# Block two in a second layout: factors found in groups, queries left unnormalized, gate units inside the attention, and the next norm begun early

## The chip, the cores and the metric

One core of a Trainium2 chip runs the whole program. The metric is the device time of one execution in microseconds. Engines are named as the profile names them: PE (matmuls; PEld is its weight load), DVE (vector), ACT (scalar), POOL (GpSimd) and SP, which only issues DMAs.

## What is computed

Two blocks in a row, each of two layers, on 512 tokens of width 1024. Block one (dilated attention, a gated recurrence and two FFNs) is not touched, except for a load near its end. Block two is this, twice:

```python
h = _rmsnorm(x, norm_g[l]); z = h @ w_in[l]
(nsa_q, nsa_kv, nsa_gate, nsa_silu, fox_qkv, fox_f, fox_silu,
 mem_q, mem_silu, merge_g) = _split(z, IN_SPLITS)
# nsa: q = rope(rmsnorm(q)); three attentions: compressed keys, selected keys, window
# fox: q and k normalized, logits + c[q] - c[k], c = cumsum(log_sigmoid(f_logit + bias))
# mem: q and k normalized, softmax(q @ k_mem) @ v_mem
# each branch: (o * silu(gate part of z)) @ w_branch, times sigmoid(merge_g), summed
x = x + merged @ w_out
```

Heads are 64 wide (memory heads 128), so a tile of 128 rows holds two heads. Every head norm needs a mean of squares for each token and head.

## The kernel before

Activations lie feature by token, [128, 8, 512]. All weights come as 434 units of [128, 1024] in a fixed order (`unit_order`). SP loads a unit, POOL splits it into a high and a low part (`w_hi`, L1848; `w_lo`, four quarters, L1852), and PE multiplies high by high, high by low and low by high: 24 matmuls of 512 columns (L331 to L333) for a full unit. Three units are in flight. Each engine runs its own list of instructions in order; semaphores join them.

A layer of block two has four stages.

**Projections** (`pe_projections` and its twins on ACT and DVE). 35 units in slots m = 0 to 34, the products in banks m % 3. Eight of the slots (memory keys and values) have 256 columns in place of 512. 22 slots carry a head norm. For each of them ACT copies and squares the bank (L1175, L1178), PE sums the squares by token (L1113, "sums"), DVE finds the factor by 13 or 14 dependent tiny instructions (`dve_rsqrt`, L438 to L456, tile `ep_nar`), widens it (L1269, `ep_wide`), PE transposes it into bank 6 (L1125, "spread") and DVE multiplies (L1253). There is one set of sums in bank 7 at a time: PE waits for slot m's factor before it sums the next. Seven slots are then rotated (L1132, L1258 to L1261). Value slots are scaled by DVE (L1228) and transposed by PE (L1138). Woven between the slots: the compression of keys and values (64 matmuls each, L1326), the norm of the memory, and some 35 steps that make the forget term. What comes when is set by `later` and by generators, one or two steps a slot.

**Attention** (`pe_attend` and twins). Four chunks, n = 0 to 3, of 36 tasks. A task is a tile of 128 queries, one head, one kind. PE makes the logits, DVE finds the maximum, ACT the exponentials, PE transposes them two steps later, ACT copies them out, PE multiplies by the values four steps later (L1563), DVE stores with the factor five steps later. Queries of one head stand in a tile whose other half is zero (`nsa_q_half`), staged by DVE for each chunk. After a chunk the pipeline is emptied, three tiles of output are transposed back (L1521) and copied by ACT (L1595).

**Gates** (`pe_silu` and twins). 12 units; DVE scales, ACT takes SiLU (L1675), DVE multiplies by the attention's output (L1690), and ACT and DVE split into high and low.

**Merge**. 24 + 12 units, then 8 units of `w_out`, whose results DVE adds to the residual `x_res` (L1764). The next layer begins when the last of them is added (`layer_begins`).

## Time and profile before

| | us |
|---|---|
| median of 3 runs | 3389.7 (3380.18 to 3391.31) |
| the profiled execution, time / span | 3390.8 / 3389.3 |
| layer 0 of block two: start 1690.6, first rotation 1746.8, attention 2018.4, gates 2236.8, merge 2303.3 | |
| layer 1: start 2546.1, first rotation 2582.5, attention 2855.1, gates 3073.0, end 3389.3 | |

The stage times are read from the trace, from the last instruction of one stage to the first of the next on PE; the start of a layer is the end of the last matmul before it. The profile's PE time contains modelled ends: a matmul's row reaches over the beginning of the next, so a stretch can show more than PE does at its peak. In a window's row the stretch and its length come first, then the busy time of PE, PEld, DVE, ACT and POOL with their instructions, the granted clock, the DMA share and GB/s. The clock stands as a share of 2.4 GHz; 0.50 is 1.2 GHz.

### The profile page before, as it was taken

The page shows a single profiled execution, that of the slowest core. Times are in us where ns is not written, and L with a number is a line of the kernel's source. Part 1 is how long each engine was busy: PE and PEld are TensorE (multiplying, and loading weights), DVE is VectorE, ACT ScalarE, POOL GpSimd, SP SyncE. Part 2 cuts the span into 40 slices and gives each one's busy share as a digit, 9 for nine tenths or more (in the row PEclk, how much of TensorE's full clock was granted, in tenths as well). Part 3 has the DMA queues.
Part 4 walks back from the last instruction along what each step waited for, and adds up shares of the span by engine and source line. Part 5 has one row for each costly group of instructions (what it writes and reads, how often), then busy time and mean ns, then how long its engine had stood idle before and what let it go on. Part 6 is the DMA issues. An engine that isn't in the chain of part 4 may idle for free.

```text
span 3389.3 us, 42390 instructions
## 1 busy us (share of the span) xinstructions
PE 3157.9 (93%) x15466; PEld 2576.6 (76%) x15474; DVE 1654.8 (49%) x3680; ACT 792.4 (23%) x1755; POOL 1933.4 (57%) x2206
## 2 busy tenths in 40 slices
PE   7999998899998889999978799999998889999999
PEld 6777777788887767888767677788887767778887
DVE  2333334476603756663056666653325766665232
ACT  1111111222201422221021016641002112663100
POOL 5555553699976777998744540047774454005775
PEclk9999999899998999999978889999998888999999
DMA  3222221222231221222231220012223121001222
GB/s 138 89 87 84 95 91 44 69 94 94 94 100 63 74 81 69 94 94 97 100 108 49 70 69 1 1 48 96 94 100 112 50 75 56 2 1 62 95 95 86
DMA packets 66445, 255.74 MB, mean 75 GB/s; under 512 B 7616, under 2 KB 8128, under 8 KB 64320
## 3 DMA queue, kind: packets, MB, share of 16 engines
q1 hardware_dynamic: 62496, 227.57, 20.0%
q10 hardware_dynamic: 3744, 25.47, 2.1%
q8 instruction: 125, 2.05, 0.2%
q14 instruction: 80, 0.66, 0.1%
HBM read 250.91 MB, written 2.10 MB: 75 GB/s over the span
## 4 chain that ended last, share of the span: by engine, by line
PE 87%; DVE 8%; issue 2%; ACT 2%; POOL 1%; DMA 0%; ACTq 0%; DVEq 0%; POOLq 0%
PE bank L331 21%; PE bank L332 21%; PE bank L333 21%; PE bank L1563 4%; PE bank L1540 3%; PE bank L1553 2%; PE bank L369 2%; PE bank L359 1%; PE bank L597 1%; PE bank L361 1%; PE bank L360 1%; PE bank L1535 1%; PE bank L1113 1%; PE bank L569 1%; PE bank L585 1%
## 5 line engine op out<-in xcount | busy, mean ns | idle before, releaser
L1852 POOL TENSOR_TENSOR w_lo<-w_raw,w_hi 128x256 fp32r<-128x256 f32 x1736 | 1411.5, 844 | 36.2
L1848 POOL TENSOR_SCALAR w_hi<-w_raw 128x1024 fp32r<-128x1024 f32 x434 | 479.1, 1104 | 1372.8 <-PE bank L333 1216.4
L331 PE MATMUL bank<-in_hi,w_hi 128*128 128x512 f32 x1408 | 566.1, 402 | 5.3 <-ACT factor_wide L422 2.8
L332 PE MATMUL bank<-in_lo,w_hi 128*128 128x512 f32 x1408 | 560.0, 398 | 0.0
L333 PE MATMUL bank<-in_hi,w_lo 128*128 128x512 f32 x1408 | 559.4, 397 | 0.0
L331 PE MATMUL bank<-z_hi,w_hi 128*128 128x512 f32 x976 | 397.8, 408 | 1.6 <-DVE silu L1688 1.6
L332 PE MATMUL bank<-z_lo,w_hi 128*128 128x512 f32 x976 | 389.7, 399 | 0.0
L333 PE MATMUL bank<-z_hi,w_lo 128*128 128x512 f32 x976 | 388.7, 398 | 0.0
L331 PEld LDWEIGHTS bank<-in_hi,w_hi 128*128 128x128 f32 x1408 | 266.7, 189 | 68.2 <-ACT factor_wide L422 3.5
L333 PEld LDWEIGHTS bank<-in_hi,w_lo 128*128 128x128 f32 x1408 | 266.3, 189 | 65.0
L332 PEld LDWEIGHTS bank<-in_lo,w_hi 128*128 128x128 f32 x1408 | 266.5, 189 | 61.5
L331 PEld LDWEIGHTS bank<-z_hi,w_hi 128*128 128x128 f32 x976 | 190.2, 195 | 42.5 <-DVE silu L1688 2.4
L333 PEld LDWEIGHTS bank<-z_hi,w_lo 128*128 128x128 f32 x976 | 189.1, 194 | 41.2
L332 PEld LDWEIGHTS bank<-z_lo,w_hi 128*128 128x128 f32 x976 | 190.0, 195 | 39.4 <-issue 1.0
L551 DVE TENSOR_TENSOR out_squares<-out_squares,square 128x512 f32<-128x512 f32 x32 | 32.4, 1012 | 292.1 <-ACT square L542 292.0
L1624 DVE TENSOR_REDUCE at_st<-bank 128x1 f32<-128x256 f32 (+4 forms) x288 | 119.8, 416 | 75.6 <-PE bank L1541 32.8
L332 PE MATMUL bank<-ffn_hidden_lo,w_hi 128*128 128x512 f32 x384 | 149.4, 389 | 0.0
L333 PE MATMUL bank<-ffn_hidden_hi,w_lo 128*128 128x512 f32 x384 | 149.4, 389 | 0.0
L331 PE MATMUL bank<-ffn_hidden_hi,w_hi 128*128 128x512 f32 x384 | 149.4, 389 | 0.0
L1591 ACT ACTIVATE at_p<-bank,at_st 128x256 f32<-128x256 f32 (+4 forms) x288 | 134.5, 467 | 40.6 <-DVE at_st L1635 33.8
L1584 ACT ACTIVATE at_pt<-bank 128x256 f32<-128x256 f32 (+4 forms) x288 | 113.0, 392 | 98.1 <-PE bank L1553 96.1
L1748 DVE TENSOR_TENSOR o_all<-bank,z_factor_wide 128x512 f32<-128x512 f32 x48 | 33.1, 690 | 192.1 <-PE bank L333 192.1
(398 smaller groups left out, 5323.6 us busy)
## 6 DMA issues: line engine op xcount, KB each, us to landing
w_raw<-in_units SPq DMA_DIRECT2D x434, 512.0 KB, 3.4
bias<-in_bias ACTq DMA_DIRECT2D x8, 1152.0 KB, 5.2
o_all<-in_cmp_w ACTq DMA_DIRECT2D x4, 2048.0 KB, 8.4
x_res<-in_x ACTq DMA_DIRECT2D x4, 512.0 KB, 9.0
mem_in<-in_mem ACTq DMA_DIRECT2D x2, 1024.0 KB, 4.8
out<-x_res ACTq DMA_DIRECT2D x1, 2048.0 KB, 6.3
consts<-in_consts ACTq DMA_DIRECT2D x1, 710.5 KB, 3.8
both_layers_cols<-in_layer_cols ACTq DMA_DIRECT2D x2, 140.5 KB, 4.0
```

The source lines that it names most:

```text
L331: pe.matmul(out, hi[:, w], rh, start=start and n == 0, stop=False)
L332: pe.matmul(out, hi[:, w], rl, start=False, stop=False)
L333: last = pe.matmul(out, lo[:, w], rh, start=False, stop=stop and n == len(tiles) - 1)
L369: m = pe.matmul(bank[:, t:t + 1], sq[:, t * P:t * P + P], c.ones[:, 0:1], start=first and t == 0, stop=last, skip_group_check=True)
L1540: pe.matmul(b[:, 0:t.keys], c.nq[j][:, q], k[:, 0:t.keys], start=True, stop=False)
L1553: m = pe.matmul(b[0:t.rows, s * P:s * P + P], p[:, s * P:s * P + t.rows], c.ident[:, :], is_transpose=True)
L1563: m = pe.matmul(o, pt[0:t.rows, s * P:s * P + P], v, start=s == 0, stop=s == len(values) - 1)
L1584: c.s.turned_out.on(act.activation(c.at_pt[t.index % 3][0:t.rows, 0:t.tiles * P], c.bank[3 + t.index % 2][0:t.rows, 0:t.tiles * P], ACT.Co ...
L1591: c.s.exponentials.on(act.activation(c.at_p[t.index % 3][:, 0:t.keys], c.bank[t.index % 3][:, 0:t.keys], ACT.Exp, scale=t.scale, bias=st[: ...
L1624: dmax = step.on(dve.reduce_max(st[:, 0:1], c.bank[t.index % 3][:, 0:t.keys], AX_X))
L1848: d = c.s.unit_hi.on(pool.tensor_scalar(c.w_hi[s][:, :], c.w_raw[s][:, :], 1.0, 0.0, ALU.mult, ALU.add))
L1852: last = pool.tensor_tensor(c.w_lo[s][:, w], c.w_raw[s][:, w], c.w_hi[s][:, w].bitcast(F32), ALU.subtract)
```

## The change

- **Banks and groups.** Products go to banks m % 4. The slots of a head norm form five groups (6, 4, 4, 4 and 4 slots). Each slot's sums have columns of their own in bank 7, and the factor is found once a group, on up to 48 columns (`dve_group_factors`). ACT, not DVE, widens (`act_widen`), and the gain goes into ACT's copy from the bank.
- **Queries.** The eight query slots of nsa and mem get no spread and no multiplication. Their factor is used in the attention as the scale of the exponential and of the maximum (`nsa_scale`, `mem_scale`, one column a task).
- **Keys.** The nsa keys are written twice, each head between zeros (`sel_k[0]`, `sel_k[1]`), so queries aren't staged.
- **Attention.** One pipeline of 144 tasks, never emptied. The 12 gate units are cut in halves of 12 matmuls and placed after steps 10, 14, 19, 23, 28 and 32 of each chunk. The outputs are transposed back, gated and split during the next chunk. The first six merge units begin in the tail.
- **Next norm.** The norm of layer 1 starts chunk by chunk as `w_out` results are added; that of layer 0 as the last results of block one are added. The squares have eight buffers. The constants are loaded before block one's last units.
- **Output** goes out in four DMAs rather than one. Tiles of 512 bytes or more start at multiples of 512 bytes.

```diff
 def pe_projections(pe, c, layer):
-    pe.wait_ge(*layer_begins(c, layer))
     pe_norm_start(pe, c, z, [("z", layer, m) for m in range(3)])
...
-                pe.wait_ge(*c.free[m % 3])
+                pe_free(pe, c, m % 4)
...
-        c.free[7] = c.s.factor_found["ep", layer, s.m]
+    elif what == "factors":
+        c.free[7] = c.s.sums_read[layer, s.last]
...
+    groups = [Group(c, which, out, 64 * i) for i, which in
+              enumerate(([3, 4, 5, 6, 7, 8], [11, 12, 14, 15], [13, 16, 19, 22], [23, 24, 25, 26], [27, 28, 29, 30]))]
+SPREAD = {10: 3, 11: 4, 17: 11, 18: 12, 19: 14, 20: 15, 28: 23, 29: 24, 30: 25, 31: 26, 32: 27, 33: 28, 34: 29, 35: 30}
+ROPE = {1: 0, 11: 3, 12: 4, 13: 5, 14: 6, 15: 7, 16: 8}
...
+def act_widen(act, c, layer, s):
+    act.wait_ge(*c.s.factor_found["ep", layer, s.group.last])
...
+        if s.kind == "k":
+            first, second = (c.sel_k, c.win_k)[s.m - 3]
+            dve.memset(second[0:HD, :], 0.0)
+            dve.memset(first[HD:P, :], 0.0)
+            dve.tensor_tensor(second[HD:P, :], c.ep_rope[0][HD:P, :], c.ep_rope[1][HD:P, :], ALU.add)
...
+CHUNK, TASKS, STAGE = 36, 144, 5
+GATE_STEPS = {10: (0, 0), 14: (0, 4), 19: (1, 0), 23: (1, 4), 28: (2, 0), 32: (2, 4)}
+GATE_OUT = {18: (0, 0), 27: (0, 1), 0: (1, 2)}
+BACK = {5: 0, 7: 1, 9: 2}
+BACK_HI, BACK_LO = {6: 0, 8: 1, 10: 2}, {7: 0, 9: 1, 11: 2}
+TAIL_MERGE = {144: (0, 1), 145: (1, 2), 146: (2, 0), 147: (3, 3), 148: (4, 4)}
...
 def act_attend(act, c, layer):
+        if n < 4 and step == STAGE:
+            act_stage(act, c, layer, n, tasks)
+        if n and step == 3:
+            act_silu(act, c, layer, n - 1)
...
+def act_silu(act, c, layer, n):
+    for j in range(3):
+        act.wait_ge(*c.s.evicted["silu", layer, 3 * n + j])
+        s = c.o_all[:, n + 4 * j, :]
+        c.s.act_step.on(act.activation(s, s, ACT.Silu), ("silu", layer, n, j))
...
 def dve_merge(dve, c, layer):
+        if layer == 0 and n:
+            dve_norm_chunk(dve, c, following, n - 1)
```

The rows below are the instructions in program order, not times. On DVE, in the projections of layer 0, behind slot 3's product there stood a whole chain for that slot (the numbers behind names are buffers):

```order
L1396 TENSOR_TENSOR o_all<-cmp_src_k,both_layers_cols 64x16x31 x4
L438 SCALAR_TENSOR_TENSOR ep_nar_165<-bank,z_factor_square_141 128x8
L440 TENSOR_SCALAR ep_nar_165<-ep_nar_165 128x8
L442 TENSOR_SCALAR ep_nar_166<-ep_nar_165 128x8
L444 TENSOR_SCALAR ep_nar_164<-ep_nar_166 128x8
L447 TENSOR_TENSOR ep_nar_166<-ep_nar_164 128x8
...
L456 TENSOR_TENSOR ep_nar_164<-ep_nar_164,z_factor_by_head 128x8
L1269 COPY ep_wide_170<-ep_nar_164 128x512
L427 SCALAR_TENSOR_TENSOR mem_lo<-mem_in,both_layers_cols,mem_hi 128x256 x2
L438 SCALAR_TENSOR_TENSOR ep_nar_168<-bank,z_factor_square_141 128x8
```

In the changed kernel the first such chain comes behind slot 8, for six slots at once:

```order
L1493 TENSOR_TENSOR o_all<-cmp_src_v,both_layers_cols 64x16x31 x4
L451 SCALAR_TENSOR_TENSOR mem_lo<-mem_in,both_layers_cols,mem_hi 128x256 x2
L1281 MEMSET fox_base 128x256
L1282 MEMSET fox_rhs 128x256
...
L1342 SCALAR_TENSOR_TENSOR group_m<-bank,z_factor_square_141 128x48
L1344 TENSOR_SCALAR group_m<-group_m 128x48
L1346 TENSOR_SCALAR group_a<-group_m 128x48
...
L1357 TENSOR_TENSOR group_r_183<-group_r_183,z_factor_by_head 128x48
L1360 TENSOR_SCALAR nsa_scale<-group_r_183 128x32
L1361 TENSOR_SCALAR nsa_minus<-group_r_183 128x32
```

The chain has the same length and stands there five times a layer, not 22 times. On ACT, between chunk 0 and chunk 1 of the attention of layer 0, the list was:

```order
L1591 ACTIVATE at_p_205,at_st_214<-bank,at_st_214 128x256
L1584 ACTIVATE at_pt_207<-bank 128x256
L1584 ACTIVATE at_pt_208<-bank 128x256
L1595 ACTIVATE o_all<-bank 128x512 x3
L1576 ACTIVATE fox_q_half_217<-fox_q 64x512
L1576 ACTIVATE fox_q_half_218<-fox_q 64x512
L1591 ACTIVATE at_p_203,at_st_209<-bank,at_st_209 128x31
```

And now, at steps 3 to 6 of chunk 1:

```order
L1728 ACTIVATE at_p_230,at_st_161<-bank,at_st_161,nsa_scale 128x512
L1758 ACT_TABLE_LOAD
L1758 ACTIVATE o_all<-o_all 128x512 x3
L1721 ACTIVATE at_pt_235<-bank 128x128
L1728 ACT_TABLE_LOAD
L1728 ACTIVATE at_p_231,at_st_162<-bank,at_st_162,nsa_scale 128x128
L1721 ACTIVATE at_pt_233<-bank 128x512
L1728 ACTIVATE at_p_232,at_st_163<-bank,at_st_163,nsa_scale 128x512
L1750 ACTIVATE fox_q_first<-fox_q 64x512
L1750 ACTIVATE fox_q_second<-fox_q 64x512
L1721 ACTIVATE at_pt_234<-bank 128x128
```

Three SiLUs and two table loads now stand between an exponential and the next. On PE, at the same place, the pipeline was emptied:

```order
L1563 MATMUL bank<-mem_v,at_pt_207 128x128 x2
L1563 MATMUL bank<-mem_v,at_pt_208 128x128 x2
L1521 MATMUL bank<-ident,o_rows_221 128x128 x4
L1521 MATMUL bank<-ident,o_rows_222 128x128 x4
L1521 MATMUL bank<-ident,o_rows_223 128x128 x4
L1530 MATMUL bank<-cmp_k,nsa_q_half_215 128x31
L1531 MATMUL bank<-mask_bf,ident_bf 128x31
```

Now the next chunk's logits stand between the last values of the old one:

```order
L1672 MATMUL bank<-mem_k,mem_q 128x256
L1693 MATMUL bank<-ident,at_p_230 128x128 x3
L1708 MATMUL bank<-fox_v,at_pt_234 128x64 x3
L1669 MATMUL bank<-cmp_k_156,nsa_q 128x31
L1670 MATMUL bank<-mask_bf,ident_bf 128x31
L1693 MATMUL bank<-ident,at_p_231 128x128 x2
L1708 MATMUL bank<-fox_v,at_pt_235 128x64 x2
```

The transposes back (L1659) come 5, 7 and 9 steps after that, one tile at a time.

## Rows read from the trace of the kernel before

**Rows 1.** The profile's page: engine totals, and the clock in 40 slices.
```profile
PE 3157.9 (93%) x15466; PEld 2576.6 (76%) x15474; DVE 1654.8 (49%) x3680; ACT 792.4 (23%) x1755; POOL 1933.4 (57%) x2206
PEclk9999999899998999999978889999998888999999
```

**Rows 2.** Windows: engines' busy time in each stage, the last chunk apart.
```profile
1746.80:2018.40 271.60, 233.64 (x1229) 199.80 (x1229) 183.41 (x466) 40.96 (x87) 133.22 (x161) 0.88 0.23 75
2018.40:2236.80 218.40, 207.98 (x1405) 163.96 (x1409) 144.99 (x717) 138.43 (x450) 0.00 (x0) 0.95 0.01 3
2236.80:2303.30 66.50, 65.72 (x291) 54.11 (x290) 33.55 (x34) 15.99 (x25) 53.37 (x56) 1.00 0.24 80
2546.10:2582.50 36.40, 27.86 (x141) 23.57 (x141) 20.19 (x32) 10.44 (x17) 14.74 (x20) 0.90 0.30 113
2582.50:2855.10 272.60, 234.12 (x1230) 199.89 (x1230) 183.57 (x466) 40.58 (x86) 133.30 (x161) 0.88 0.23 76
2186.00:2235.00 49.00, 47.72 (x339) 37.96 (x340) 34.94 (x176) 32.33 (x109) 0.00 (x0) 1.00 0.01 2
```

**Rows 3.** PE's waits from 1737 to 2018 us: total, times, longest.
```profile
PE bank L1113 <- DVE ep_nar L456: 12.8, 3, 4.9
PE bank L1138 <- DVE ep_vt L1228: 10.4, 2, 7.4
```

**Rows 4.** Windows, on the tile ep_nar alone: PE, PEld, DVE.
```profile
1746.80:2018.40 271.60, 3.91 (x24) 2.89 (x24) 97.01 (x322) 0.88 0.23 75
```

**Rows 5.** Windows of 10 us in the projections: PE, PEld, DVE, ACT, POOL, clock.
```profile
1890.00:1900.00 10.00, 5.09 (x36) 4.88 (x36) 9.09 (x20) 0.28 (x1) 6.98 (x10) 0.78 0.31 104
1920.00:1930.00 10.00, 5.25 (x14) 4.25 (x15) 6.04 (x10) 0.39 (x1) 2.51 (x4) 0.51 0.28 100
```

**Rows 6.** Timeline of PE in the projections, at the full clock.
```profile
1817.60 0.60 PE L1125 MATMUL bank<-ident,ep_wide 128*128 128x128 f32 x4
1818.04 0.95 PE L1113 MATMUL bank<-consts,ep_sq 128*128 128x2 f32 x8
1818.85 7.34 PE L1326 MATMUL bank<-o_all 128*128 128x62 f32 x64
...
1945.33 0.95 PE L1113 MATMUL bank<-consts,ep_sq 128*128 128x2 f32 x8
1946.13 0.48 PE L331 MATMUL bank<-z_hi,w_hi 128*128 128x512 f32 x1
...
1951.67 0.60 PE L1125 MATMUL bank<-ident,ep_nar 128*128 128x128 f32 x4
```

**Rows 7.** Timeline of one factor chain on DVE and POOL beside it.
```profile
1790.34 2.77 POOL L1852 TENSOR_TENSOR w_lo<-w_raw,w_hi 128x256 fp32r<-128x256 f32 x4
1792.49 0.64 DVE L447 TENSOR_TENSOR ep_nar<-ep_nar 128x8 f32<-128x8 f32 x1
1793.56 0.17 DVE L447 TENSOR_TENSOR ep_nar<-ep_nar 128x8 f32<-128x8 f32 x1
```

**Rows 8.** The chain that ended last, around the end of block one's first FFN.
```profile
1266.40 0.24 PE bank L333
1306.21 0.61 ACT factor_wide L422
```

**Rows 9.** The chain that ended last, from chunk 0 to chunk 1 of the attention.
```profile
2074.07 0.36 DVE o_rows L1656
2079.68 0.30 PE bank L1553
```

**Rows 10.** Timeline of ACT around a table load.
```profile
1835.58 0.63 ACT L777 ACTIVATE forget_work<-forget 64x512 f32<-64x512 f32 x1
1836.23 1.28 ACT L779 ACT_TABLE_LOAD   x1
1837.53 0.63 ACT L779 ACTIVATE forget_work<-forget_work 64x512 f32<-64x512 f32 x1
```

**Rows 11.** The page's DMA issues: the output.
```profile
out<-x_res ACTq DMA_DIRECT2D x1, 2048.0 KB, 6.3
```

More of the change, by code:

```diff
@@ L1062, in layer_begins @@
[L1062 to L1078 removed]
+    for i, s in enumerate([s for s in out if s.kind in ("q", "k")]):
+        s.turn = i
@@ new lines, in later, with two_turns_back @@
+def later(every, groups, m):
+    s = every[m - 1] if 1 <= m <= SLOTS_TWO else None
+    if s and s.kind in ("q", "k"):
+        yield "sums", s
+    if m in groups:
+        yield "factors", groups[m]
+    if m in SPREAD:
+        yield "spread", every[SPREAD[m]]
+    if m in ROPE:
+        yield "rope", every[ROPE[m]]
+    if s and s.kind == "rows":
+        yield "turn", s
+    if s and s.kind == "gates":
+        yield "gates", s
+def two_turns_back(every, s):
+    kinds = ("rows",) if s.kind == "rows" else ("q", "k")
+    return [x for x in every if x.kind in kinds and x.turn == s.turn - 2][0]
@@ L1159, in act_projections @@
                 c.s.rows_out.on(act.activation(s.dst, c.bank[4][:, 0:s.n].rearrange("p (t n) -> p t n", n=P), ACT.Copy), (layer, s.m))
+            if what == "spread" and s.heads == 2:
+                act_widen(act, c, layer, s)
         if m >= 3:
@@ new lines, in pe_silu_half @@
+def pe_silu_half(pe, c, layer, z, u, first):
+    key = ("silu", layer, u)
+    assert c.order[c.u] == key
+    if first == 0:
+        pe.wait_ge(*c.s.unit_split[c.u])
+        pe_free(pe, c, 7)
+    hi, lo, out = c.w_hi[c.u % SLOTS], c.w_lo[c.u % SLOTS], c.bank[7][:, :]
+    for k in range(first, first + DC // 2):
+        w = slice(k * P, k * P + P)
+        pe.matmul(out, hi[:, w], z.hi[:, k, :], start=k == 0, stop=False)
+        pe.matmul(out, hi[:, w], z.lo[:, k, :], start=False, stop=False)
+        last = pe.matmul(out, lo[:, w], z.hi[:, k, :], start=False, stop=k == DC - 1)
+    if first:
+        pe_unit_done(c, key, last)
+        c.free[7] = c.s.evicted["silu", layer, u]
@@ L1782, in pe_program @@
         pe_attend(pe, c, layer)
-        pe_silu(pe, c, layer)
         pe_merge(pe, c, layer)
```

776 lines of the change are left out of this document (427 added, 349 removed).

## The prediction

> **What bounds the kernel now.** I began with the page. PE is busy for 93% of the span and no other engine for more than 57% [rows 1], so PE's list of instructions sets the time, and only three things can move it: PE work taken away, time in which PE waits, and time in which it runs below its full clock. The clock line dips in two places, one for each layer of block two [rows 1]. So I cut block two into its stages [rows 2]. The gate stage is full (65.72 of 66.50 us, clock 1.00), and so is the merge. The projections are not: 271.60 us, of which PE is busy for 233.64, at a mean clock of 0.88, while DVE is busy for 183.41 us. In the attention PE is busy for 207.98 of 218.40 us at 0.95. Then I asked what PE waits for in the projections: mostly a factor that DVE hasn't found, or a value tile that DVE hasn't scaled because factors stand before it [rows 3]. DVE spends 97.01 us of the stage on the factor tile alone, in 322 instructions [rows 4].
>
> So the projections are held up by one engine's tiny dependent instructions, and PE pays twice: in one stretch of 10 us it was busy for 5.09 us beside a DVE busy for 9.09, and in another that waited as long the granted clock was 0.51, 1.2 GHz [rows 5].
>
> **The sum of the projections.** How long is the stage if PE never waits and keeps its clock? From the first rotation to the first logits, with durations at the full clock [rows 6]:
> - 24 units of 512 columns at 5.54 (1946.13 to 1951.67): 133.0; 8 units of 256 columns, half of that: 22.2.
> - Sums: 18 slots at 0.80 (1945.33 to 1946.13), 4 short ones at half: 16.0.
> - Compression, two at 7.3: 14.6, and 1 for its small matmuls.
> - Rotations, 7 at about 0.9 (an estimate: an fp32 product of 512 columns as four of a unit's 24 at 0.23): 6.3.
> - Spreads at 0.44 (1817.60 to 1818.04): now 14 and not 22, four of them short: 5.3. Value transposes are alike: 3.5.
> - Memory norm, eight short sums and a spread: 3.9.
>
> This makes 206 us, against 271.6 and 272.6 now [rows 2]. The eight dropped spreads are only 3.5 of the difference; some 62 is waiting and low clock.
>
> How much does the change recover? Less the widening, the chains cost DVE 91 us for 22, 4.1 each. Five chains are 21, so DVE drops by 70; ACT takes the widening (6) and has 230 us idle in the stage. The wider tile (48 columns for 8) is cheap next to 0.17 for a single instruction [rows 7]. DVE then has some 115 us of work in about 215. Added are zeros and half-tile additions for the keys, about 4 us in all. The sums have their own columns, so the wait of 12.8 us in [rows 3] has nothing left to wait for: six slots' sums pass before one chain. Where is DVE late next? In slots 11 to 16, which are short on PE (four memory units of 2.8 us) but carry six rotations (an estimate of 2.5 to 4.7 us of DVE each, three to six instructions on whole or half tiles), a group chain and two forget steps each. By the list I get about 33 us of DVE against 30 of PE there; four banks and one slot of lead take up most. I count 4 us for this, 2 at the compression, whose input DVE must first write, 2 at the memory factor, and 4.5 for the clock after the wait for the layer's factor, which stays. The stage becomes 218 us. Gain 53.6 and 54.6: **108**. If PE waits hardly at all it is 212; if DVE's lag costs as much as a third of today's loss, it is 228 to 240. I take 218 because slots 23 to 30 of the kernel before ran back to back under a heavier DVE load [rows 6].
>
> **The starts of the layers.** Layer 0: from 1690.6 to 1746.8 is 56.2 us. The change overlaps POOL's residual adds with the norm, as block one does already. There the same passage takes 40.4 us (1266.40 to 1306.82 [rows 8]), plus some 1.3 for the head factors: a gain of **14.5**. Layer 1: 36.4 us [rows 2]. Seven of the eight norm chunks now lie under `w_out`. PE goes on at once at full clock: 8 times (six matmuls of 0.23 and sums of 0.80, about 2.28 with the turnover) is 18.3, then about 10 for the factor and its spread, as now. 28.3; gain **8**. ACT's and DVE's chunks (about 0.7 each) hide under units of 5.54.
>
> **The attention with the gates inside.** The 12 units don't get cheaper: 66.5 us of PE moves, and PE is nearly full where it goes. What can be won is only today's loss. PE stood idle for 10.4 us, and 0.05 of clock is another 11. Dense, a chunk is 47 to 49 (the last one took 49.00 at clock 1.00 [rows 2]), so the four are about 192, and with the gates 258.5 against 284.9 now. Each chunk boundary cost 5.6 us from the last store to the next transpose [rows 9], which is most of it. Against this stand new costs:
> - Table loads. SiLU and exp take turns: 1.28 to SiLU, 3 times 0.63, 1.28 back [rows 10] keep ACT from exponentials for 4.5 us, and 1.3 of staging copies and 1.9 of high parts come right behind. PE has about two steps of lead (2.7 us). I take 3.3 us for each of three chunk starts: 10. In the tail, merge units cover it.
> - POOL. It splits the gate weights inside the attention, where it was idle, 4.4 us a unit (53.37 for twelve [rows 2]). A tiny DVE instruction takes 0.64 while POOL subtracts and 0.17 when it doesn't [rows 7]. Twelve bursts; between 0 and 1.5 us each (no row shows this mix), since a gate half of 2.8 us has just let DVE catch up. I take 0.4 each: 5.
> - Filling the one pipeline, and a longer chain from the scale columns: 3.
>
> The sum is 276.5 a layer; gain 8.4, twice: **17**. ACT's exps get a scale column, DVE's maximum too: under 0.1 us each, covered by PE. The zeroed keys cost PE nothing: it contracted 128 rows before as well.
>
> The Trainium skill (ScalarE: Activation LUTs, section "What ACT_TABLE_LOAD costs") charges 1.28 us for the load and as much again for a drain, 2.66 in all. The trace doesn't bear out the drain in front: the load begins 0.02 us after the ACTIVATE before it and the next one begins 0.02 behind it [rows 10]. By the page the three boundaries would cost 8 us more a layer, and the forecast would be 16 us higher.
>
> **The tail.** The output is one DMA of 6.3 us [rows 11]. Three quarters now leave early. The last quarter I put at 3.8, between a fixed part and the whole: **2.5**. Merge units and `w_out` are untouched at 5.54 each. The constants' DMAs wait inside DVE's list before block one's last units; units of 5.5 us on PE hide it.
>
> **Sum.** 108 + 14.5 + 8 + 17 + 2.5 = 150. The profiled execution took 3390.8, 1.1 above the median, so 3240.8 by it and 3239.7 against the median. I say 3240.
>
> **Rivals.**
> 1. *The attention gives its gain back* (0.17). Table loads, staging and POOL bursts fall on the same DVE and ACT steps. For it: both prices are measured [rows 7, 10] and the steps coincide. Against it: ACT is busy for 138 of 218 us. Attention with gates would take 290 to 300 us in place of 276.5: 27 to 45 more in all, about 3275.
> 2. *DVE stays the bound of slots 9 to 20* (0.15). The forget steps, rotations and compression remain, and each wait halves the clock. For it: DVE is 9 tenths busy there today [rows 5]. The stage is then 235 to 240: about 3280.
> 3. *PE runs dense almost throughout* (0.10). Projections 210, attention with gates 264: 41 less, about 3200.
> 4. *Slower* (0.04). PE's pauses at the table loads and bursts come often enough that the clock stays at 1.2 GHz in the attention. Each us of work at half clock costs one more. The forecast leaves 150 us, so with 10 for a measurable loss it decides once 160 of the 517 us of work in the two layers run at 1.2 GHz; with 200 of them the time is 3440. Against it: the last chunk kept 1.00 with small pauses [rows 2].
> 5. *Nothing is gained*, since the time goes elsewhere on PE (0.02): 3385 to 3395.
>
> The forecast itself (3215 to 3265) has 0.52. The Trainium skill (SBUF — State Buffer, section "Who interferes with whom") says that DVE and GpSimd share a pair of ports, held for a whole instruction. The trace agrees, 0.64 against 0.17 [rows 7]; it is the ground of rival 1's second part.
>
> **How the numbers follow.** The range reaches from rival 3 to rivals 1 and 2: 3195 to 3300. It leaves out 0.06 of the slower cases and the outer parts of the rivals, some 0.12. A change under 0.3% (10 us) can't be told from none, since the three runs spread over 11 us. Faster 0.93, same 0.03, slower 0.04.
>
> **What would show it.** Right: projections at 212 to 225 us with DVE under 60% and a clock above 0.95; sums that no longer wait for a factor; attention with gates at 265 to 285 and clock near 1.00; PE waiting for `at_p` 2 to 4 us at each chunk start. Wrong: an attention above 290, with maxima late during POOL's bursts; PE waiting on rotations or spreads in slots 10 to 17 for more than 10 us; a first rotation of layer 1 more than 30 us after the last `w_out`.

## The result: 3252.5 us, and where the time came from

The kernel after takes **3252.5 us** (median of four runs, 3249.7 to 3257.3) beside 3386.6 before: a ratio of 0.9607, with a 95% interval of 0.9585 to 0.9628. That is faster, and 12 us above the forecast. Its profiled execution took 3257.3 us with a span of 3255.8, where before it was 3390.8 and 3389.3. The page of the kernel after, its line for PE and its clock, answers to [rows 1]:

```profile
PE 3088.7 (95%) x15410; PEld 2553.7 (78%) x15410; DVE 1538.4 (47%) x3162; ACT 823.8 (25%) x1763; POOL 1906.6 (59%) x2206
...
PEclk9999999899999998999999999999998999999999
```

PE is fuller, DVE has shed a good part of its work, and the two dips of the clock have almost gone. The stages of the kernel after, as windows (length, then PE, PEld, DVE, ACT, POOL busy, clock, DMA share, GB/s), answer to [rows 2]: the start of layer 0, its projections, its attention, its merge with `w_out`, then the start, the projections, the attention and the merge of layer 1.

```profile
1665.90:1708.90 43.00, 30.29 (x153) 25.43 (x152) 26.86 (x45) 12.42 (x20) 27.62 (x28) 0.84 0.27 97
1708.90:1938.40 229.50, 215.93 (x1197) 185.31 (x1198) 125.02 (x224) 46.52 (x94) 139.00 (x160) 0.96 0.26 88
1938.40:2216.90 278.50, 266.03 (x1671) 214.90 (x1669) 156.82 (x731) 160.11 (x464) 47.01 (x62) 0.96 0.07 24
2216.90:2461.00 244.10, 243.11 (x1087) 201.44 (x1087) 75.61 (x98) 35.47 (x57) 178.19 (x215) 1.00 0.31 102
2461.00:2489.60 28.60, 24.76 (x141) 21.08 (x139) 12.39 (x19) 1.84 (x3) 15.95 (x20) 0.95 0.22 73
2489.60:2728.20 238.60, 226.30 (x1197) 193.93 (x1198) 124.53 (x224) 46.21 (x93) 139.03 (x160) 0.92 0.25 84
2728.20:3006.60 278.40, 264.99 (x1655) 212.95 (x1654) 155.53 (x727) 158.69 (x459) 46.00 (x61) 0.96 0.07 24
3006.60:3252.40 245.80, 244.79 (x1101) 202.72 (x1099) 70.81 (x96) 28.53 (x47) 169.51 (x207) 1.00 0.27 90
```

Set against the marks of the kernel before (1690.6, 1746.8, 2018.4, 2546.1, 2582.5, 2855.1, and 3382.3 for the end of the last matmul), the 133.5 us between the two spans come from the passages below. The last column sets the kernel after against a1 instead, the kernel before with the new layout alone, which comes first among the experiments (its marks: 1665.2, 1717.1, 1987.9, 2511.9, 2546.7, 2820.3, 3338.5, span 3345.6).

| passage | forecast gain | measured | beside a1 |
|---|---|---|---|
| block one, to 1690.6 / 1665.9 | 0 | 24.7 | -0.7 |
| start of layer 0 | 14.5 | 56.2 - 43.0 = 13.2 | 8.9 |
| projections, two layers | 108 | 42.1 + 34.0 = 76.1 | 41.3 + 35.0 = 76.3 |
| start of layer 1 | 8 | 36.4 - 28.6 = 7.8 | 6.2 |
| attention, gates, merge, `w_out`, two layers | 17 | 5.1 + 3.0 = 8.1 | 1.4 - 6.0 = -4.6 |
| tail behind the last matmul | 2.5 | 7.0 - 3.4 = 3.6 | 3.7 |
| sum | 150 | 133.5 | 89.8 |

The profiled execution of a1 was its fastest of four and that of the kernel after its slowest, so the last column is some 9 us low as a whole: by the ratios the two kernels are 98 us apart.

Three rows ask for an explanation: 24.7 us in a block whose instructions nobody touched, projections that are 32 us short of the forecast, and an attention that is 9 short.

**PE's waits** in the projections of layer 0, after (total, times, longest), answer to [rows 3]:

```profile
PE bank L1185 <- DVE ep_vt L1296: 4.2, 2, 3.5
PE bank L1173 <- DVE group_r L1357: 3.5, 1, 3.5
...
PE bank L1179 <- DVE ep_rope L1317: 1.8, 1, 1.8
PE bank L393 <- ACT mem_square L441: 1.7, 2, 1.1
PE bank L1179 <- DVE cmp_src_k L1301: 1.5, 1, 1.5
```

The sums of a slot no longer wait for a factor at all. But two waits of 3.5 us are left. The timeline of DVE shows the first: after the group's chain of factors come two steps of the forget gates, one a RECIPROCAL of 3.35 us, and only then the value tile, for which PE stands idle from 1785.8 to 1789.36.

```profile
1784.23 0.21 DVE L1357 TENSOR_TENSOR group_r<-group_r,z_factor_by_head 128x48 f32<-128x48 f32 x1
...
1784.77 0.42 DVE L811 TENSOR_SCALAR forget_work<-forget_work 64x512 f32<-64x512 f32 x1
1785.23 3.35 DVE L814 RECIPROCAL forget_work<-forget_work 64x512 f32<-64x512 f32 x1
1788.61 0.69 DVE L1296 TENSOR_TENSOR ep_vt<-bank,z_factor_wide 128x512 f32<-128x512 f32 x1
```

**ACT at the first chunk boundary** of the attention, after: the two table loads that [rows 10] gave a price for, with three SiLUs between them, hold up a turned tile (`at_pt`) and the next exponential for 4.4 us. PE waits 2.97 us for `at_p` there, and 11.3 us in six such waits over the layer's attention.

```profile
2009.07 0.19 ACT L1728 ACTIVATION_READ_ACCUMULATOR at_p<-bank,at_st,nsa_scale 128x1 f32 x1
2009.28 1.28 ACT L1758 ACT_TABLE_LOAD   x1
2010.58 1.67 ACT L1758 ACTIVATE o_all<-o_all 128x512 f32<-128x512 f32 x3
2012.15 0.26 ACT L1721 ACTIVATE at_pt<-bank 128x128 f32<-128x128 f32 x1
2012.43 1.28 ACT L1728 ACT_TABLE_LOAD   x1
2013.72 0.46 ACT L1728 ACTIVATE at_p<-bank,at_st,nsa_scale 128x128 f32<-128x128 f32 x1
```

### The profile page after: what moved, and what is told of

Read it like the earlier page. It is cut to its first block, busy times and chain, and to the rows that moved or that the text cites. A ratio compares the mean times of both kernels' runs of the same rounds, so it can differ in the third digit from the quotient of the medians.

```text
span 3255.8 us, 41911 instructions
## 1 busy us (share of the span) xinstructions
PE 3088.7 (95%) x15410; PEld 2553.7 (78%) x15410; DVE 1538.4 (47%) x3162; ACT 823.8 (25%) x1763; POOL 1906.6 (59%) x2206
## 3 DMA queue, kind: packets, MB, share of 16 engines
q8 instruction: 125, 2.05, 0.3%
## 4 chain that ended last, share of the span: by engine, by line
PE 86%; DVE 8%; ACT 3%; issue 2%; DMA 0%; POOL 0%; ACTq 0%; DVEq 0%; POOLq 0%
PE bank L355 20%; PE bank L357 20%; PE bank L356 20%; PE bank L1708 4%; PE bank L1693 2%; PE bank L1682 2%; PE bank L393 2%; PE bank L1646 2%; PE bank L383 1%; PE bank L1648 1%; PE bank L1647 1%; PE bank L621 1%; PE bank L385 1%; PE bank L384 1%; PE bank L1677 1%
## 5 line engine op out<-in xcount | busy, mean ns | idle before, releaser
L2022 POOL TENSOR_TENSOR w_lo<-w_raw,w_hi 128x256 fp32r<-128x256 f32 x1736 | 1383.2, 828 | 36.2
L356 PE MATMUL bank<-in_lo,w_hi 128*128 128x512 f32 x1408 | 550.2, 391 | 0.0
L355 PE MATMUL bank<-z_hi,w_hi 128*128 128x512 f32 x784 | 317.5, 405 | 0.0
L357 PE MATMUL bank<-z_hi,w_lo 128*128 128x512 f32 x784 | 309.0, 394 | 0.0
L356 PE MATMUL bank<-z_lo,w_hi 128*128 128x512 f32 x784 | 308.9, 394 | 0.0
L355 PEld LDWEIGHTS bank<-z_hi,w_hi 128*128 128x128 f32 x784 | 149.8, 191 | 31.9 <-issue 1.5
L357 PEld LDWEIGHTS bank<-z_hi,w_lo 128*128 128x128 f32 x784 | 149.2, 190 | 32.4
L356 PEld LDWEIGHTS bank<-z_lo,w_hi 128*128 128x128 f32 x784 | 149.6, 191 | 31.7 <-issue 2.0
L575 DVE TENSOR_TENSOR out_squares<-out_squares,square 128x512 f32<-128x512 f32 x32 | 32.5, 1017 | 278.5 <-ACT square L566 278.4
L1693 PE MATMUL bank<-ident,at_p 128*128 128x128 f32 (+1 forms) x608 | 121.1, 286 | 24.3 <-ACT at_p L1728 23.8
L1728 ACT ACTIVATE at_p<-bank,at_st,nsa_scale 128x31 f32<-128x31 f32 (+2 forms) x192 | 103.1, 537 | 43.6 <-DVE at_st L1802 42.3
```

Source lines behind the costliest of these rows:

```text
L355: pe.matmul(out, hi[:, w], rh, start=start and n == 0, stop=False)
L356: pe.matmul(out, hi[:, w], rl, start=False, stop=False)
L357: last = pe.matmul(out, lo[:, w], rh, start=False, stop=stop and n == len(tiles) - 1)
L1693: m = pe.matmul(b[0:t.rows, s * P:s * P + P], p[:, s * P:s * P + t.rows], c.ident[:, :], is_transpose=True)
L1728: c.s.exponentials.on(act.activation(c.at_p[t.index % 3][:, 0:t.keys], c.bank[t.index % 3][:, 0:t.keys], ACT.Exp, scale=exp_scale(c, t), b ...
L2022: last = pool.tensor_tensor(c.w_lo[s][:, w], c.w_raw[s][:, w], c.w_hi[s][:, w].bitcast(F32), ALU.subtract)
```

## The experiments

Eleven kernels were run. Each one's ratio is to runs of the kernel before on its own chip; the kernel before took 3383 to 3392 us (medians) there, so a difference between two ratios is good to about 0.003, some 10 us. A stage of the profile is the finer measure, but it is one execution: block one, in the same layout, took 1690.6 us in the trace of the kernel before and 1680.2 in that of a2.

### Block one: where a tile starts

The only part of the change that reaches block one's tiles is the layout: `Area.take` now rounds the start of every tile of 512 bytes and more up to a multiple of 512. Grouped by form (busy us, mean ns), the kernel before has two speeds for the same 128x512 product, and the kernel after has one. Before:

```profile
L333 PE MATMUL bank<-in_hi,w_lo 128*128 128x512 f32 x1408 | 559.4, 397 | 0.0
...
L333 PE MATMUL bank<-ffn_hidden_hi,w_lo 128*128 128x512 f32 x384 | 149.4, 389 | 0.0
```

After:

```profile
L357 PE MATMUL bank<-in_hi,w_lo 128*128 128x512 f32 x1408 | 550.4, 391 | 0.0
...
L357 PE MATMUL bank<-ffn_hidden_hi,w_lo 128*128 128x512 f32 x384 | 149.4, 389 | 0.0
```

A row's mean reaches over its neighbour; the distance from start to start is 0.234 us on `in_hi` before (16 starts from 99.65 to 103.40) and 0.227 after (10 from 101.04 to 103.31). With 7220 matmuls in block one in both traces and the clock at 0.97 in both, PE was busy 24.4 us less.

**a1_aligned_before.** The kernel before with the new `take`. To make it fit, the constants' tiles take the order and place that they have in the change, and an unused gap goes.

```diff
-        t = self.nc.alloc_sbuf_tensor_at(name, shape, dt, offset=self.at)
+        step = 512 if size >= 512 else 32
+        self.at = -(-self.at // step) * step
+        t = self.nc.alloc_sbuf_tensor_at(name, shape, dt, offset=self.at)
```

> The kernel before, with one thing of the change alone: tiles of 512 bytes and more start at multiples of 512 bytes. It bears on the 24.7 us by which block one ended earlier in the kernel after, though none of its instructions changed. Theory A, the place of the moving operand: in the trace of before the split matmuls on in_hi and in_lo last 397 to 402 ns and follow each other every 0.2335 us, those on ffn_hidden 389 ns and 0.2275 us; 4224 of them times 0.006 us is 25 us, and 768 on oz and u give 4.6 us more, so about 3357 us (3352 to 3362), block one ending near 1666. Theory B, something else of the change (the earlier load of the constants, what the end of the program leaves to the next execution) or the execution itself: 3386 us, no change.

Measured: 3351.4 us, ratio 0.9895 (0.9874 to 0.9915), so 29 to 43 us less, at and just beyond the fast end of what was expected. Block one ends at 1665.2, as in the kernel after. The layout alone does it; theory B falls.

**a2_block_one_unaligned.** The kernel after, with block one and the weight tiles back in their old places (steps of 32 bytes from 1152).

```diff
-        step = 512 if size >= 512 else 32
+        step = 512 if size >= 512 and self.aligned else 32
...
+        Area.default = False
         a = Area(nc, 1152)
...
+        Area.default = True
-        self.block_two(a.at)
+        self.block_two(-(-a.at // 512) * 512)
```

> The kernel after, with the tiles of block one put back to steps of 32 bytes (in_hi again 288 bytes past a multiple of 512); block two is left as it is. Theory A: block one ends near 1691 again instead of 1666, the time is 3277 us (3273 to 3281), and in_hi matmuls last 397 ns. Theory B: 3252 us, no change.

Measured: 3295.1 us, 0.9732 (0.9709 to 0.9756), 43 more than the kernel after and well past the 3281 at which the expectation ended. The reason is in block two, whose tiles were left at multiples of 512:

```profile
L361 PE MATMUL bank<-ffn_hidden_lo,w_hi 128*128 128x512 f32 x384 | 149.4, 389 | 0.0
...
L361 PE MATMUL bank<-o_lo,w_hi 128*128 128x512 f32 x192 | 75.8, 395 | 0.0
...
L362 PE MATMUL bank<-u_hi,w_lo 128*128 128x512 f32 x96 | 37.9, 395 | 0.0
...
L362 PE MATMUL bank<-z_hi,w_lo 128*128 128x512 f32 x784 | 312.9, 399 | 0.0
```

`o_lo`, `u_hi` and `z_hi` start at a multiple of 512 and are slow (`z_hi` has 394 ns in the kernel after); `ffn_hidden` starts 384 past one and is fast. The 3024 products on `z` were fast in the kernel before as well, 0.227 us from start to start where this kernel has 0.233, so a2 slows down more than the change had sped up, and its 43 us are not what the layout gave. So it isn't the place of the moving tile alone. What this kernel also moved back are the weight tiles, to 128 past a multiple of 512.

**a3_in_moved.** The kernel before, `in_hi` and `in_lo` moved from 288 to 384 past a multiple of 512; the stage's tiles behind them land on a multiple of 512.

```diff
         self.rate = a.take("log_a_rate", [P, DC])
+        a.at += 96
...
-        stage = a.at
+        stage = a.at = a.at + 32
```

> The kernel before with two gaps in the layout and nothing else: in_hi and in_lo move by 96 bytes, from 288 to 384 past a multiple of 512 bytes, and the tiles behind stay at multiples of 128. Theory A in its narrow form (a moving operand that starts at a multiple of 128 bytes is read at 0.2275 us for 512 columns, another at 0.2335): 3361 us (3357 to 3365), block one ending near 1666. Theory A in its wide form, that only multiples of 512 do: 3386 us, no change. Theory B: 3386 us.

Measured: 3370.3 us, 0.9954 (0.9942 to 0.9966), a median of ten runs, between the two theories. `in_hi` became fast and `ffn_hidden`, now at a multiple of 512, slow:

```profile
L334 PE MATMUL bank<-in_hi,w_lo 128*128 128x512 f32 x1408 | 552.9, 393 | 0.0
...
L334 PE MATMUL bank<-ffn_hidden_hi,w_lo 128*128 128x512 f32 x384 | 151.7, 395 | 0.0
```

Both forms of theory A fall. What fits all rows is the distance between the start of the weight tile and that of the moving tile, modulo 256 bytes. With weights at 128, the moving tiles at 384 are fast and those at 0, 64 and 288 slow; with weights at 0, those at 0 are fast. The sum fits too: 4224 products gain 0.006 us each and some 1630 (`ffn_hidden` and the tiles that share its place) lose as much, which leaves 16 us, and 12 to 20 were measured. This became theory E, tried on the weights alone.

**a4_weights_128** and **a5_weights_256.** The kernel after, only the ring of weight tiles placed otherwise:

```diff
-        self.w_raw = [a.take(f"w_raw{s}", [P, D]) for s in range(SLOTS)]
-        self.w_hi = [a.take(f"w_hi{s}", [P, D], F32R) for s in range(SLOTS)]
-        self.w_lo = [a.take(f"w_lo{s}", [P, D], F32R) for s in range(SLOTS)]
+        self.w_raw, self.w_hi, self.w_lo = ([nc.alloc_sbuf_tensor_at(f"{name}{s}", [P, D], dt, offset=1152 + (3 * i + s) * 4096) ...
```

(1280 in place of 1152 in the second.)

> The kernel after with one thing changed: the nine weight tiles start 128 bytes past a multiple of 512 bytes, where they lay in the kernel before; every other tile stays at a multiple of 512. Theory E, from the four kernels so far: 512 columns take 0.2275 us where weight tile and moving tile start at the same residue of 256 bytes (128 and 384 in the kernel before, 0 and 0 in the kernel after), and 0.2335 where they differ (128 with 288, 64 or 0). Then all of some 10,000 split matmuls slow down by 0.0053 to 0.006 us: 53 to 60 us more, 3305 to 3312 us. Theory A, that only the place of the moving tile counts: no change, 3252 us.

> As the run before, with the weight tiles 256 bytes past a multiple of 512. Theory E: no change against the kernel after, 3252 us (3248 to 3257), matmuls of 512 columns at 389 ns. Theory G, that both must start at the same residue of 512 bytes: 3305 to 3312 us, as with 128.

Measured: 3291.8 us, 0.9707 (0.9683 to 0.9732) with 128, and 3254.6 us, 0.9603 (0.9584 to 0.9622) with 256. Theory E holds in sign and place. All the long forms of the first are slow, as its rows show:

```profile
L357 PE MATMUL bank<-in_hi,w_lo 128*128 128x512 f32 x1408 | 559.2, 397 | 0.0
...
L355 PE MATMUL bank<-ffn_hidden_hi,w_hi 128*128 128x512 f32 x384 | 151.6, 395 | 0.0
```

Its size was over-reckoned: 39 us and not 53 to 60. The trace (an execution of 3298.7 us) shows where some of it went. Block one took 28 us more than in the kernel after, and the two passages from the first logits to the last matmul 9 and 5 more, but the projections of layer 1 took 4 less (234.7 for 238.7, clock 0.94 for 0.92): a stretch at low clock that the kernel after has there (below, "Layer 1's extra 9 us") didn't come. How the rest splits is not shown.

### The projections: VectorE in slots 9 to 18

**s2_two_stalls.** The kernel after, with both 3.5 us waits attacked by order.

```diff
-SPREAD = {10: 3, 11: 4, 17: 11, 18: 12, 19: 14, 20: 15, ...
+SPREAD = {10: 3, 11: 4, 18: 11, 19: 12, 20: 14, 21: 15, ...
...
-        if m >= 9:
-            next(forget, None)
-            next(forget, None)
         if m < SLOTS_TWO:
             dve_epilogue(dve, c, layer, every[m], every, zm if every[m].memory else z)
+        if m >= 9:
+            next(forget, None)
+            next(forget, None)
```

> The kernel after, with VectorE doing a slot's epilogue ahead of the steps of the forget gates instead of behind them, and with TensorE asking for the four factors of the memory keys one slot later (slots 18 to 21 for 17 to 20). It bears on the projections, 229.5 and 238.6 us where 218 was forecast. Theory C: TensorE's two waits of 3.55 us (for ep_vt behind the 3.35 us RECIPROCAL, for group_r behind the chain of 8-column operations at 0.65 us each) are stalls that cost their own length and some 1 to 3 us of low granted clock behind each: both layers together 14 us plus 2 to 8 us, so 3234 us (3229 to 3239). Rival D: VectorE is the bound over these slots, with 19.2 of 20 us busy in 1810 to 1830, and the wait only moves to the next instruction that it serves: gain under 4 us, 3249 to 3253 us.

Measured: 3257.8 us, 0.962 (0.9601 to 0.9639): nothing gained. Its waits in layer 0:

```profile
PE bank L1185 <- DVE ep_vt L1296: 4.4, 1, 4.4
...
PE bank L1173 <- DVE sel_k L1311: 1.7, 1, 1.7
...
PE bank L1173 <- DVE group_r L1357: 1.4, 1, 1.4
```

The wait for `group_r` shrank, the one for `ep_vt` is a single one of 4.4 and a new one for `sel_k` stood beside them. In this trace DVE was busy for 18.97 and 19.23 us of the two stretches of 20 from 1790. Rival D came: an engine so full wasn't helped by its order.

**f1_forget_late.** The kernel after, with the forget gates' steps taken out of that stretch.

```diff
-        if m >= 9:
-            next(forget, None)
-            next(forget, None)
+        if m >= 18:
+            for _ in range(3):
+                next(forget, None)
```

> The kernel after, with the 42 VectorE steps of the forget gates done three a slot from slot 18 on instead of two a slot from slot 9 on. The last kernel moved two waits and they came back a slot later, for VectorE was busy 19.0 and 19.2 of 20 us in the two stretches around them. Theory D, VectorE is the bound of slots 9 to 18: with about 18 us of its work taken out of 1785 to 1850, the waits for ep_vt (3.55), group_r (3.55) and ep_rope (1.8) go, with 2 to 3 us of low clock behind them in each layer: 9 us a layer, 3234 us (3228 to 3242). Rival: the waits are a matter of order alone, and what VectorE then meets at slots 18 to 31 (the groups of factors at 23, 27 and 31) takes as much: 3249 to 3256 us.

Measured: 3238.9 us, 0.9555 (0.9532 to 0.9578), 13.6 us under the kernel after by the medians. The two projections of its trace:

```profile
1707.90:1930.10 222.20, 213.08 (x1197) 182.47 (x1198) 128.13 (x224) 46.54 (x94) 139.29 (x160) 0.98 0.27 91
2481.70:2713.50 231.80, 224.17 (x1197) 192.32 (x1198) 127.41 (x224) 46.21 (x93) 139.90 (x160) 0.92 0.26 87
```

7.3 and 6.8 us less than 229.5 and 238.6, which is the whole gain. Theory D holds in size, but not in all it named: the wait for `ep_vt` fell from 4.2 to 2.1 and that for `ep_rope` went, while the one for `group_r` stayed, at 3.4. Of the 7.3 us, some 4 are waits, the rest is clock (0.96 to 0.98). From 1785 to 1850 DVE was busy for 48.2 us and not 53.2, so far less than the 18 us expected left that stretch: a PE that waits less brings other work into it.

**p1_split_a_quarter.** Why is a chain slow? In the trace of after, operations on 8 to 48 columns take 0.19 or about 0.65 us. This kernel leaves out three of GpSimd's four low-half subtractions for the units of the projections. What it computes there is not the reference's, since those units are multiplied with stale low halves; it serves to time the rest.

```diff
-        for quarter in range(4):
+        for quarter in range(1 if c.order[u][0] == "z" else 4):
```

> The kernel after with three of GpSimd's four low-half subtractions left out for the units of the projections (w_lo of those units keeps what an earlier unit left there, so the projections' values are not the reference's; everything else runs as it did). Theory P, sharing with GpSimd: VectorE operations of 8 to 48 columns that take 0.19 us alone take 0.58 to 0.68 in the trace of after while GpSimd works, so a chain of 14 takes 8 us instead of 3. With GpSimd's 139 us in a layer's projections cut to some 60, the waits for group_r (3.5) and ep_vt (3.5) shrink to under 2 together, with less low clock behind: 7 to 10 us a layer, 3234 us (3230 to 3242). Rival: the chains slow down by what GpSimd's copy of w_hi does and not by its subtractions, or the waits are set by the RECIPROCAL of 3.35 us alone: 3246 to 3254 us.

Measured: 3235.3 us, 0.9561 (0.954 to 0.9582), 17 us under the kernel after. The chain's three repeated lines over the projections of layer 0 (count, busy, mean ns), in the kernel after:

```profile
L1351 DVE TENSOR_TENSOR group_a<-group_r 128x32 f32<-128x32 f32 (+3 forms) x15 | 6.5, 436 | 0.5
...
L1353 DVE SCALAR_TENSOR_TENSOR group_a<-group_a,group_m 128x32 f32<-128x32 f32 (+3 forms) x15 | 5.7, 378 | 0.5
L1355 DVE SCALAR_TENSOR_TENSOR group_r<-group_a,group_r 128x32 f32<-128x32 f32 (+3 forms) x15 | 5.6, 373 | 0.5
```

and in this kernel:

```profile
L1351 DVE TENSOR_TENSOR group_a<-group_r 128x32 f32<-128x32 f32 (+3 forms) x15 | 2.8, 188 | 0.5
L1353 DVE SCALAR_TENSOR_TENSOR group_a<-group_a,group_m 128x32 f32<-128x32 f32 (+3 forms) x15 | 2.8, 187 | 0.5
L1355 DVE SCALAR_TENSOR_TENSOR group_r<-group_a,group_r 128x32 f32<-128x32 f32 (+3 forms) x15 | 2.8, 187 | 0.5
```

Every one of the 45 now takes 0.17 to 0.21 us, and DVE's busy time in the stage falls from 125.0 to 103.8 us with the same 224 instructions: some 21 us of DVE's list are GpSimd's doing. The wait for `group_r` is gone, but those for `ep_vt` come to 4.4, so the two did not shrink to under 2 as expected. The Trainium skill (SBUF — State Buffer, section "Who interferes with whom") says that the two engines share ports, and the runs agree, 0.65 against 0.19. The projections take 225.0 and 225.1 us here, so 4.5 and 13.5 less; the larger share is in layer 1, on which more below.

The traces say more than the sum. Of the 90 operations of these lines in both layers of the kernel after, 51 start with GpSimd idle and take 0.17 to 0.21 us; 37 start beside a subtraction, with medians of 0.65 to 0.67; and two start beside GpSimd's copy of `w_hi` and take 1.00 and 1.01, so the copy holds them up as well. One of the two, on 8 columns, and the operation behind it, which falls into the gap between a copy that ends at 1829.12 and a subtraction that begins at 1829.20:

```profile
1828.12 1.00 DVE L1351 TENSOR_TENSOR group_a<-group_r 128x8 f32<-128x8 f32 x1
1829.16 0.17 DVE L1353 SCALAR_TENSOR_TENSOR group_a<-group_a,group_m 128x8 f32<-128x8 f32 x1
```

This chain, for the memory keys, lasts from 1824.27 to 1832.19, 7.9 us, and PE's second wait of 3.55 us is for its end. In p1 none of the 90 starts beside GpSimd.

**n1_norm_late.** The kernel after, with layer 1's norm begun only when the last tile is added.

```diff
-            act.wait_ge(*c.s.residual_added["w_out", 0, k])
+            act.wait_ge(*c.s.residual_added["w_out", 0, DC - 1])
...
-        if layer == 0 and n:
-            dve_norm_chunk(dve, c, following, n - 1)
     if layer == 0:
-        dve_norm_chunk(dve, c, following, DC - 1)
+        for n in range(DC):
+            dve_norm_chunk(dve, c, following, n)
```

> The kernel after with one part of the change undone: the squares and the low halves of layer 1's norm are made when the last w_out sum has been added, instead of tile by tile between them. The forecast gave this part 8.1 us (36.4 us before, 28.3 forecast, 28.6 seen from the last w_out unit to the first rotation). Theory: 3260 us (3258 to 3264). Rival: with eight buffers for the squares the late norm runs without TensorE's sums in between and is as fast, so that the order gives nothing: 3252 us.

Measured: 3254.4 us, 0.9611 (0.9584 to 0.9638): no difference that can be told. In the trace the passage from the last add (2461.06) to the first rotation is 31.3 us for 28.6:

```profile
2463.64 0.50 PE L383 MATMUL bank<-z_hi,w_hi 128*128 128x512 f32 x1 [2.62 <-DVE z_lo L451]
...
2492.34 2.05 PE L1179 MATMUL bank<-cmp_src_k,consts 128*128 128x512 f32 x2 [1.51 <-DVE cmp_src_k L1301]
```

So of the 7.8 us that the start of layer 1 gained, the early order gives 2.7. The other 5 stay when it is undone; a1 took 34.8 us there for 36.4, so up to 1.6 of them may be layout. What this kernel keeps are the eight buffers for the squares (ACT needs 1.13 us a tile there and never waits, where two buffers made it wait for PE's sums), a PE whose clock stays up, and a first wait of 2.6 us where the kernel before stood for 4.7. I didn't take these three apart.

### The attention: SiLU and exp

**t1_tanh.** The kernel after, with the gate written through tanh, one unit at each of the steps 3, 5 and 7.

```diff
-        if n and step == 3:
-            act_silu(act, c, layer, n - 1)
+        if n and step in TANH:
+            act_silu(act, c, layer, n - 1, TANH[step])
...
-        c.s.act_step.on(act.activation(s, s, ACT.Silu), ("silu", layer, n, j))
+    c.s.act_step.on(act.activation(c.fox_k[:, n, :], c.o_all[:, n + 4 * j, :], ACT.Tanh), ("silu", layer, n, j))
...
+def dve_tanh(dve, c, layer, n, j):
+    h = c.o_all[:, n + 4 * j, :]
+    dve.wait_ge(*c.s.act_step["silu", layer, n, j])
+    c.s.dve_step.on(dve.scalar_tensor_tensor(h, c.fox_k[:, n, :], 1.0, h, ALU.add, ALU.mult), ("silu", layer, n, j))
```

> The kernel after, with the SiLU of the gates as h * (1 + tanh h), h being half the gate: tanh in place of SiLU on ScalarE, one unit at each of steps 3, 5 and 7 of the next chunk instead of three at step 3, and one more VectorE operation of 0.69 us for each of the 24. Theory H, what attention and gates lack against the forecast (278 us and the tail behind it, where 276.5 with all gates was forecast) is the burst on ScalarE at each chunk's start, two table loads of 1.28 us and three SiLUs, 4.2 us in a row, behind which TensorE waits 3.0 and 0.5 us for at_p: if tanh shares a table with exp, 3 us or more at each of 6 chunk starts and 1 to 2 us at each of two ends go, 3232 us (3226 to 3238). Rivals: the 24 operations on VectorE cost what the tables give, 3248 to 3256 us; or tanh has a table of its own, with two loads for each unit instead of for three, and the kernel is slower, 3262 to 3275 us.

Measured: 3233.3 us, 0.9541 (0.9522 to 0.9559), 19 us under the kernel after. At the same boundary, ACT:

```profile
2008.90 0.19 ACT L1729 ACTIVATION_READ_ACCUMULATOR at_p<-bank,at_st,nsa_scale 128x1 f32 x1
2009.00 0.62 ACT L1761 ACTIVATE fox_k<-o_all 128x512 f32<-128x512 f32 x1
2009.52 0.27 ACT L1722 ACTIVATE at_pt<-bank 128x128 f32<-128x128 f32 x1
```

No table load stands between exp and tanh, here or at any other tanh of this trace: the two share a table. The part from the first logits of a layer to the next layer's first rotation took 543.0 us for 551.2, and in layer 1 the part to the end of the span took 517.2 for 527.6. PE's waits for `at_p` in layer 0 fell from 11.3 to 3.7 us. Against that the trace shows 4.4 us of waits for `o_all` that were 0.9: the longer list of DVE takes back a part. A further 5.6 us came from layer 1's projections (233.0 for 238.6), which the edit doesn't touch; they are not the tanh's. (The three make 24 us between the two profiled executions, of which that of the kernel after was 5 us above its median.)

**c1_combined.** Tanh gates, late forget gates and the memory factors one slot later, in one kernel: the edits of t1 and f1 with the `SPREAD` line of s2.

> Three edits on the kernel after at once: the tanh gates, the forget gates from slot 18 on, and the four memory key factors asked for one slot later (18 to 21), now that VectorE is no longer the bound there. The tanh gates alone gave 19.2 us and the late forget gates 13.6; they lie in different stages, and the run with late forget gates kept a wait of 3.4 us for group_r in each layer. Theory D and H: the gains add, and the 3.4 us go with 1 to 2 us of clock behind each, 19 + 14 + 9 = 42: 3211 us (3206 to 3218). Rival: the wait for group_r moves on as it did before (gain 33, 3219 us), or what the clock gives in one stage it takes in the next, 3222 to 3226 us.

Measured: **3217.1 us**, 0.9505 (0.9484 to 0.9526), the fastest kernel here, 35 us under the kernel after. It lies at the upper end of the expected range, 2 us from the rival's 3219, so the time alone doesn't decide between them. The gains of t1 and f1 add (32.8 by the medians, 35.4 here; the difference is less than the runs tell apart). The wait for `group_r` in layer 0 is down to 0.4, and the projections are 1.3 and 5.1 us shorter than in f1:

```profile
1703.32:1924.21 220.89, 213.49 (x1198) 182.10 (x1199) 128.11 (x224) 46.44 (x94) 140.05 (x160) 0.98 0.27 91
...
2466.49:2693.22 226.73, 220.38 (x1197) 188.59 (x1198) 127.17 (x224) 46.16 (x93) 140.80 (x160) 0.94 0.27 89
```

So the `SPREAD` edit, part of s2 that brought nothing while VectorE was full, goes with a wait that is gone once it isn't; what its 3 us bring to the whole stays inside the noise.

## Why the forecast was right, and where it wasn't

The forecast was 3240 us, and 3252.5 was measured, inside the range. It deserves less credit than that: two errors of opposite sign met. Nor did all of its own signs of being right come: the projections were to take 212 to 225 us at a clock above 0.95 and took 229.5 and 238.6 at 0.96 and 0.92, and the attention was to run near 1.00 and ran at 0.96.

**What it missed.** "Merge units and `w_out` are untouched at 5.54 each", and a block one in which nothing changes. These steps failed. The diff showed the new `take`, and the rows of the kernel before had the two speeds in them; I read neither. The layout is worth 29 to 43 us by a1, so of the 134 us gained about a quarter is layout. The rest of the change is worth some 98 us, the distance of the ratios 0.9895 and 0.9607, two thirds of the 150 forecast for it. Without the layout it would have stood near 3288 us, still inside the range: that the result fell so near 3240 is luck.

**What held.** The start of layer 0 (13.2 us for 14.5), that of layer 1 (7.8 for 8) and the tail (3.6 for 2.5) came close to what was worked out. Beside a1 the starts are 8.9 and 6.2, so a part of the first, 4 us in these single executions, may be layout too. For layer 1 the size was right and the reason wrong: "seven of the eight norm chunks now lie under `w_out`" gives 2.7 us of it (n1). The sums wait for no factor, and PE's waits for `at_p` at chunk starts were 3.0 us, inside the 2 to 4 named.

**The projections**, 229.5 and 238.6 us for 218. The step that failed is "I get about 33 us of DVE against 30 of PE there; four banks and one slot of lead take up most. I count 4 us for this". The two stalls of 3.55 and the one of 1.8 make 8.9 us. The count of DVE's work was near (125 us for 115), but not its distribution: I had priced a chain at its mean of 4.1, and the one on which PE waited, with GpSimd at work almost throughout, took 7.9; all in all GpSimd's doing is 21 of the 125 us (p1). f1 shows the place: with the forget gates moved out of slots 9 to 17, 7 us of each layer go. This is rival 2 in mechanism, with half to all of its price.

The other part is the clock. I had allowed 4.5 us for it behind the first wait only. In windows of 20 us over layer 0 the clock was 0.91 to 0.93 in three and 0.83 in one; what lies under 1.00 there makes 8 us, and in this layer every such stretch has a wait in it or just ahead of it.

**Layer 1's extra 9 us** are clock too. The 64 narrow products of the compression took 12.06 us in the kernel after and 7.34 in t1, and the unit behind them began at 0.43 us a matmul in place of 0.23:

```profile
2505.29 12.06 PE L1424 MATMUL bank<-o_all 128*128 128x62 f32 x64
...
2519.81 0.63 PE L356 MATMUL bank<-z_lo,w_hi 128*128 128x512 f32 x1
```

The same in t1:

```profile
2497.20 7.34 PE L1424 MATMUL bank<-o_all 128*128 128x62 f32 x64
```

In p1, where the chain for the layer's factor is short, the first rotation ran at 1.10 us and not 2.05, the clock was 0.96 in both layers, and both took 225 us. That points at the idle passage ahead of the stage, but doesn't show it: n1 lengthens that passage by 2.7 us and its projections of layer 1 take the same 238. No wait stands near the low stretch either. The clock was 1.00 from 2495 to 2505, 0.73 to 2510 and 0.50 to 2520, and PE's only waits from 2492 to 2520 are of 0.2 and 0.3 us. Those 64 products take 11.5 to 12.2 us in layer 1 of the kernel after, a5, s2, f1, n1 and c1, not in that of a2, a4, p1 and t1, and in layer 0 of no run. Why is open.

**The attention**, 8.1 us for 17, of which the layout gives 5.8 by count (960 matmuls on `o` and `u` times 0.006), leaving 2; beside a1's single execution nothing is left. The price of a boundary was right: 3.3 us for each of three, and PE's waits for `at_p` are 9.7 us in layer 0 without the first task's 1.6. The step that failed is "what can be won is only today's loss", in which I counted the stage's idle time and lost clock as won. Neither came back. Over attention and gates of layer 0, PE stood idle for 11.2 of 284.9 us before and for 12.5 of 278.5 after, and the clock was 0.96 both times. Behind each boundary it fell again, to 0.83, 0.70 and 0.79 over 10 us, which makes 6.8 us a layer. t1, which takes the boundaries' waits away, got 8 to 10 us a layer back at a clock of 1.00, in spite of twelve more operations on DVE. Rival 1 named this mechanism and over-priced it (290 to 300 us for the stage). The drain that the Trainium skill (ScalarE: Activation LUTs, section "What ACT_TABLE_LOAD costs") puts beside a load isn't in this trace either: 0.02 us stand between the last exponential and the load, and 0.02 between the load and the SiLU.

Rivals 3, 4 and 5 did not come: PE was not dense, the clock in the attention was 0.96, and nothing went elsewhere.

## What to carry to other kernels

Read a layout edit as a change of every instruction that touches the tiles: compare one form's pace between two tiles of the same shape before you call a stage untouched. Where an engine is busy for 19 of 20 us in a stretch, moving its instructions about inside the stretch gives nothing; take work out of it, and then the small edits begin to pay. A stall of PE can cost more than its length: around the waits of 3 us at the chunk boundaries the clock was 0.70 to 0.83 for 10 us. So the place for a table load or a long RECIPROCAL is where PE has work in hand. And when an edit changes two things at once, measure one of them alone on the old kernel: a1 is the kernel beside which the rest of this change has to be read.

## What the runs showed of the hardware

- A product in fp32r (the type of the high and low halves) of 128x128 by 128x512 starts every 0.227 us when the weight tile and the moving tile start at the same residue of 256 bytes in a partition, and every 0.232 to 0.234 when they differ (differences of 128, 160 and 192 were seen; smaller ones were not, at this size). It is the difference that counts, not the place of either: 256 bytes more for the weights changed nothing (3254.6 us), 128 cost 39 us of 3252.
- Tanh and exp need no table load between them (t1); SiLU and exp need one of 1.28 us each way.
- A 128-partition VectorE operation on 8 to 48 columns takes 0.19 us, with GpSimd's subtractions running beside it 0.65, and beside its copy 1.00 (two cases); with three quarters of the subtractions left out, 45 of 45 took 0.17 to 0.21.
- The granted clock can fall to 0.50 while PE has no wait longer than 0.3 us: it did so in layer 1 (2510 to 2520), where 64 products of 62 columns took 12.06 us in place of 7.34.
